# Loading each expert weight tile as two half transfers, in a two-model kernel whose experts stream from HBM

## The chip, the cores and the metric

The kernel runs on one core of one Trainium2 chip. The metric is the device time of one execution in microseconds (us), lower is better. The core has engines that run side by side: TensorE (PE in the profile; its weight loads PEld), VectorE (DVE), ScalarE (ACT), GpSimd (POOL) and SyncE (SP), which here only issues transfers; 16 DMA engines carry out what SP and POOL issue. All data are float32.

## The reference

The reference is a two-layer model followed by a second two-layer model, on 256 tokens of 1024 features. The change touches only the mixture of experts at the end of each of the second model's two layers:

```python
for g in range(N_GROUPS):            # 4 groups of 8 experts
    a = jnp.einsum('td,edf->tef', t, w_gate[sl])   # [256,1024] x [1024,512] an expert
    u = jnp.einsum('td,edf->tef', t, w_up[sl])
    act = jax.nn.silu(a) * u * combine[:, sl, None]
    out = out + jnp.einsum('tef,efd->td', act, w_down[sl])   # [512,1024] an expert
```

`combine` is nonzero for two experts of each token. Each expert has three weight matrices (gate, up, down) of 2 MB, so a layer reads 96 tiles of 2 MB, whichever tokens go where.

## The kernel before

Every engine has a program of its own, written out by hand, and waits on semaphores. A dictionary of names per semaphore (`Signal`) gives the value to wait for; `then_inc` attaches an increment to an instruction.

**Weights.** All weights go through one ring `W` of slots of 2 MB (16 KB in each of 128 partitions): six in `wring`; in the expert stage three more in `AR` (`W.widen`), nine in all. The SP program is the list of all transfers in the order of use. `fill` takes the next slot of the ring, waits until the tile that lay in it has been read (`bank`, `after`, `W.free`), and issues the transfer, which adds 16 to the slot's own semaphore (`slots`, s_w0 to s_w8). SP goes through its list strictly in order. A gate, up or down tile of an expert (`expert`) is laid out as `(p k) n -> p k n`: partition p gets k successive rows of the matrix, 16 KB that lie together in HBM and in the partition.

**Experts.** A layer takes the path `sparse` if no expert has more than 32 tokens, and it does on these inputs (the path `dense`, also edited, is not run). For each expert, in order, the PE program runs `up(ex)`: gate, then up, each 8 matmuls of 512 columns in four row groups of 32 (a float32 matmul stands twice in the trace, so 16 records a tile); `scatter(ex-1)`, which adds the result of the expert before into the output; `inner(ex)`, which folds and turns the products; every second expert `gather` for the next two; and `lower(ex)`, 8 matmuls with the down tile. The last matmul on a tile adds to `experts_read`, which is what SP waits for.

**Around it.** The first nine tiles of a layer's experts are fetched while the layer's mixers and router still run; then the ring is full and SP waits for the first gate tile to be read. After the last expert's tiles SP goes on with the next layer's matrices. Expert 31's up tile is number 94 of the 96 (counted from 0), its down tile number 95.

Of the kernel before, what the change touches and what calls it, by code (L numbers as in the profile page):

```python
# [16 lines left out]
NSLOT = 6  # L17
# [142 lines left out]
class Ring:  # L160
# [35 lines left out]
        kept = self.freed.setdefault(name, [])  # L196
        kept += [x for x in events if x not in kept]

    def ended(self, name):

        return self.freed.get(self.before.get(name), ())


def after(e, ring, name):

    for sig, key in ring.ended(name):
        e.wait_ge(sig, key)


# [84 lines left out]
def build(nc, t, out):  # L294
# [31 lines left out]
    def dma(name):  # L326
        return sig(name, 16)

    slots = [dma(f"w{i}") for i in range(NSLOT + 3)]
    W = Ring([wring[:, i * SLOT:(i + 1) * SLOT] for i in range(NSLOT)] + [AR[:, ARENA - i * SLOT:ARENA - (i - 1) * SLOT] for i in (2, 1, 3)], 3)  # L330
    PA, PB = Ring(banks[0:4]), Ring(banks[4:8])

# [49 lines left out]
    def tok(m):  # L382
        return slice(m * 128, m * 128 + 128)
# [118 lines left out]
    def blocks(place, kt, n):  # L502
        return place[:, 0:kt * n].rearrange("p (k n) -> p k n", k=kt)
# [59 lines left out]
    def sync(e):  # L563
        def fill(name, parts):
            place = bank(e, W, name)
            for dst, src in parts(place):
                e.dma_start(dst, src).then_inc(slots[W.where[name]], name)

# [2 lines left out]

        def expert(name, src, kt, n):

            fill(name, lambda place: [(blocks(place, kt, n), src.rearrange("(p k) n -> p k n", p=128))])

        def memory(layer):
            fill(("mem", layer), lambda place: [(pair(place[:, 2048:4096]), t["mem"][0].rearrange("(a p) d -> p a d", p=128))])
# [27 lines left out]
        c, c1, c2 = dma("c"), dma("c1"), dma("c2")  # L605
# [67 lines left out]
    def tensor(e):  # L673
        turned = sig("norm_mm")

        def place(name):

            e.wait_ge(slots[W.where[name]], name)
            return W[name]

        def weights(name, kt, n):
            return blocks(place(name), kt, n)

        def norm_half(tag, m):

# [774 lines left out]
        def sparse(layer):  # L1460

            done, vect, act = sig(f"moe_mm{layer}"), sig(f"moe_v{layer}"), sig(f"moe_a{layer}")
            read = sig(f"experts_read{layer}")
            PB = path_rings("sparse", layer)
            _, HG, SWT, GC, UC, AT, YS, _ = moe_rings(layer)

            def up(ex):
                p, x = ex // 2, ex % 2
                e.wait_ge(act, ("g", p))
                e.wait_ge(vect, ("g", p))  # L1470
                for name in ("gate", "eup"):
                    wx = weights((name, layer, ex), 8, 512)
                    ps = bank(e, PB, (name, ex))
                    for i in range(2):
                        for q in range(4):
                            k = 2 * q + i
                            ins = e.matmul(ps[32 * q:32 * q + 32, :], HG[p][:, k, 32 * x:32 * x + 32], wx[:, k, :], i == 0, i == 1)
                    ins.then_inc(read, (name, ex))
                    W.free((name, layer, ex), (read, (name, ex)))

            def inner(ex):

                ps = bank(e, PB, ("t", ex))
                for n, (tile, ready) in enumerate(((GC[ex], (act, ("gate", ex))), (UC[ex], (vect, ("eup", ex))))):
                    e.wait_ge(*ready)
                    for f in range(4):
                        c = 128 * n + 32 * f
                        ins = e.matmul(ps[:, c:c + 32], tile[:, f, :], C("fold", 32), True, True)
                ins.then_inc(done, ("t", ex))

            def lower(ex):
                wd = weights(("edown", layer, ex), 4, 1024)
                y = bank(e, PB, ("y", ex))
                e.wait_ge(vect, ("act", ex))
                for i in range(2):
                    for c in range(2):
                        for h in range(2):
                            r, f = 64 * c + 32 * h, 2 * h + i
                            ins = e.matmul(y[r:r + 32, :], AT[ex][:, f, :], wd[:, f, c * 512:c * 512 + 512], i == 0, i == 1)
                ins.then_inc(read, ("edown", ex))  # L1500
                W.free(("edown", layer, ex), (read, ("edown", ex)))

            def scatter(ex):
                p, x = ex // 2, ex % 2
                e.wait_ge(act, ("w", p))
                e.wait_ge(*((sig(f"join_v{layer}"), "end") if ex == 31 else (vect, ("y", ex))))
                for m in range(2):
                    for c in range(2):
                        r = slice(64 * c, 64 * c + 64)
                        ins = e.matmul(PA[("moe", layer), m, c][:, :], SWT[p][r, x, tok(m)], YS[ex][r, :], False, ex == 31)  # L1510
                if ex == 31:
                    ins.then_inc(sig(f"join_mm{layer}"), "end")
                else:
                    ins.then_inc(done, ("sc", ex))

            for ex in range(32):
                up(ex)
                if ex:
                    scatter(ex - 1)
                inner(ex)  # L1520
                if ex % 2 and ex < 31:
                    gather(layer, ex // 2 + 1)
                lower(ex)
            scatter(31)

        def dense(layer):

            done, vect, act = sig(f"dense_mm{layer}"), sig(f"dense_v{layer}"), sig(f"dense_a{layer}")
            read = sig(f"experts_read{layer}")
            PB = path_rings("dense", layer)  # L1530
            GAS, CR = dense_rings(layer)
            e.wait_ge(sig(f"moe_v{layer}"), ("g", 0))
            e.wait_ge(sig(f"moe_a{layer}"), ("w", 0))
            for m in range(2):
                for c in range(2):

                    e.matmul(PA[("moe", layer), m, c][:, 0:128], bc(C("strip", 1), 128), IDENT, False, True)
                    ps = bank(e, PB, ("ht", m, c))
                    for j in range(4):
                        k = 4 * c + j  # L1540
                        ins = e.transpose(ps[:, j * 128:j * 128 + 128], XN[:, m, k * 128:k * 128 + 128], IDENT)
                    ins.then_inc(done, ("ht", m, c))
            e.wait_ge(act, ("ht", 1, 1))
            for ex in range(32):
                ps = bank(e, PB, ("cr", ex))
                for m in range(2):
                    ins = e.matmul(ps[:, tok(m)], bc(CB[:, m, ex:ex + 1], 128), IDENT, True, True)
                ins.then_inc(done, ("cr", ex))
                wg, wu = (weights((name, layer, ex), 8, 512) for name in ("gate", "eup"))
                for f in range(4):  # L1550
                    ps = bank(e, PB, ("up", ex, f))
                    for j, wt in enumerate((wg, wu)):
                        for k in range(8):
                            ins = e.matmul(ps[:, j * 256:j * 256 + 256], wt[:, k, f:512:4], HT[:, k, :], k == 0, k == 7)
                        if f == 3:
                            ins.then_inc(read, (("gate", "eup")[j], ex))
                    if f < 3:
                        ins.then_inc(done, ("up", ex, f))
                wd = weights(("edown", layer, ex), 4, 1024)
                e.wait_ge(vect, ex)  # L1560
                for f in range(4):
                    for m in range(2):
                        for c in range(2):
                            ins = e.matmul(PA[("moe", layer), m, c][:, :], GAS[ex][:, f, tok(m)], wd[:, f, c * 512:c * 512 + 512],
                                           ex == 0 and f == 0, ex == 31 and f == 3)
                ins.then_inc(read, ("edown", ex))
            for c in range(2):
                ps = bank(e, PB, ("gate", c))
                e.matmul(ps[:, :], bc(IDENT[:, 64 * c:64 * c + 1], 128), experts_gate(layer), True, True).then_inc(done, ("gate", c))
            for m in range(2):  # L1570
                for c in range(2):
                    cs = slice(c * 512, c * 512 + 512)
                    e.wait_ge(sig(f"join_v{layer}"), "end")
                    e.matmul(PA[("moe", layer), m, c][:, :], IDENT, XN[:, m, cs], True, False)
                    ins = e.matmul(PA[("moe", layer), m, c][:, :], IDENT, X[:, m, cs], False, True)
            ins.then_inc(sig(f"join_mm{layer}"), "end")
# [1634 lines left out]
```

## Time and profile before

| | |
|---|---|
| device time, median of 3 runs | 2466.88 us (2464.61 to 2468.08) |
| the profiled execution | 2466.74 us, of which the span of the trace is 2464.9 us |
| PE busy / DVE / ACT | 2225.2 / 1084.9 / 588.8 us |
| granted TensorE clock, mean | 0.965 of full speed |
| DMA | 651.32 MB, 264 GB/s over the span |
| expert stages | about 1303 to 1745 us (layer 0) and 2009 to 2453 us (layer 1) |

Busy shares of TensorE come from modelled ends of pipelined matmuls and say little alone. What is to be read is what each engine waits for and, in the expert stages, what the DMA engines do. A packet is one contiguous piece moved by one DMA engine; the packets of a few bytes are the semaphore increments at the end of a transfer (16 of them for each transfer).

### The profile page before, as it was taken

To read this page: it belongs to the slowest core of one execution; us is meant where nothing else is said; L and a number is where in the kernel's file an instruction comes from. 1 tells how busy PE (TensorE), PEld (TensorE's weight loads), DVE (VectorE), ACT (ScalarE), POOL (GpSimd) and SP (SyncE) were. 2 spreads that over 40 slices of the span, in tenths; PEclk is the share of its full clock that TensorE was granted. 3 is DMA by queue.
4 is the path that set the end of the run, shared out by engine and by line. 5 is a ranking of instruction groups with operands and counts; after the bars stand their busy time and mean duration, and the time that the engine had idled before them with its cause. 6 is when DMAs were issued, how large, how long until landed. Compare 5 with 4: busy or idle time off the path is not lost.

```text
span 2464.9 us, 31938 instructions
## 1 busy us (share of the span) xinstructions
PE 2225.2 (90%) x12996; PEld 1453.2 (59%) x12996; DVE 1084.9 (44%) x2397; ACT 588.8 (24%) x1304; POOL 58.5 (2%) x88
## 2 busy tenths in 40 slices
PE   8999999999999999999998977878799989878776
PEld 7888869846865897468764433333568744333332
DVE  4764458883464688443443222222334342222222
ACT  4331423001243320032622111111314421111111
POOL 0010000001000000002000000000002000000000
PEclk9999999999999999999999999998899989999998
DMA  8221244496923646844258999999743559999996
GB/s 313 103 78 69 86 163 164 179 370 195 321 103 140 219 154 226 307 158 139 103 238 345 427 428 427 427 428 427 292 159 115 204 213 427 428 427 427 428 427 285
DMA packets 140910, 651.32 MB, mean 264 GB/s; under 512 B 6970, under 2 KB 13418, under 8 KB 116048
## 3 DMA queue, kind: packets, MB, share of 16 engines
q1 hardware_dynamic: 138336, 642.13, 66.0%
q0 software_dynamic: 2416, 7.02, 1.2%
q8 instruction: 107, 1.75, 0.3%
q14 instruction: 51, 0.42, 0.0%
HBM read 647.81 MB, written 1.31 MB: 263 GB/s over the span
## 4 chain that ended last, share of the span: by engine, by line
PE 61%; DMA 24%; DVE 10%; ACT 3%; issue 1%; DVEq 0%; ACTq 0%
PE ps L106 59%; DMA wring<-in_w_up 24%; DVE wring L129 2%; PE ps L109 2%; DVE AR L125 2%; DVE AR L129 1%; ACT AR L115 1%; ACT L115 1%; DVE wring L125 1%; DVE AR L120 1%; DVE AR L133 0%; ACT HT L115 0%; ACT wring L115 0%; DVE XN L121 0%; ACT MN L115 0%
## 5 line engine op out<-in xcount | busy, mean ns | idle before, releaser
L106 PE MATMUL ps<-HT,wring 128*128 128x256 f32 (+1 forms) x2848 | 532.0, 345 | 5.0 <-DVE wring L125 4.0
L106 PEld LDWEIGHTS ps<-HT,wring 128*128 128x128 f32 x2848 | 466.4, 193 | 62.7 <-issue 6.6
L106 PE MATMUL ps<-wring,AR 128*32 128x512 f32 (+3 forms) x1376 | 346.7, 614 | 18.4 <-DVE AR L125 17.2
L106 PE MATMUL ps<-wring,MN 128*32 128x512 f32 (+1 forms) x1504 | 241.3, 659 | 91.5 <-DMA wring<-in_w_up 79.8
L115 ACT ACTIVATE AR<-ps 128x128 f32<-128x128 f32 (+6 forms) x234 | 94.6, 404 | 721.2 <-PE ps L106 663.8
L106 PEld LDWEIGHTS ps<-wring,AR 128*32 128x32 f32 (+1 forms) x1376 | 134.8, 150 | 177.9 <-issue 176.0
L125 DVE TENSOR_TENSOR AR<-ps,AR 128x512 f32<-128x512 f32 (+4 forms) x200 | 100.5, 503 | 264.5 <-ACT AR L115 165.8
L106 PEld LDWEIGHTS ps<-wring,MN 128*32 128x32 f32 (+1 forms) x1504 | 68.1, 122 | 246.8 <-DMA wring<-in_w_up 120.7
L106 PE MATMUL ps<-AR 128*128 128x128 f32 (+5 forms) x1400 | 195.2, 393 | 13.5 <-DVE AR L125 10.8
L141 DVE COPY HT<-ps 128x512 f32<-128x512 f32 x64 | 44.3, 691 | 317.4 <-PE ps L106 317.4
L106 PEld LDWEIGHTS ps<-AR 128*128 128x128 f32 (+4 forms) x1400 | 137.5, 173 | 50.1 <-issue 36.5
L106 PEld LDWEIGHTS ps<-CS,HT 128*128 128x128 f32 x1024 | 119.1, 191 | 48.8 <-issue 48.8
L115 ACT ACTIVATE HT<-ps 128x512 f32<-128x512 f32 x112 | 66.9, 597 | 298.5 <-PE ps L106 297.0
L106 PE MATMUL ps<-XN,wring 128*128 128x128 f32 x1056 | 130.1, 275 | 3.0 <-DVE wring L125 2.0
L129 DVE SCALAR_TENSOR_TENSOR wring<-wring,CC 128x512 f32<-128x512 f32 x168 | 126.3, 752 | 6.0
L106 PE MATMUL ps<-CS,HT 128*128 128x32 f32 x1024 | 126.2, 277 | 0.0
L106 PEld LDWEIGHTS ps<-XN,wring 128*128 128x128 f32 x1056 | 123.7, 192 | 3.7 <-DVE wring L125 2.4
L106 PE MATMUL ps<-XN,AR 128*128 128x128 f32 (+1 forms) x656 | 114.4, 415 | 0.8 <-DVE AR L125 0.8
L106 PE MATMUL ps<-AR,MN 128*32 128x512 f32 (+1 forms) x704 | 86.5, 592 | 13.6 <-DMA AR<-in_w_gate 13.6
L125 DVE TENSOR_TENSOR MN<-ps,AR 128x512 f32<-128x512 f32 x64 | 44.3, 691 | 117.3 <-PE ps L106 117.3
L115 ACT ACT_TABLE_LOAD x66 | 84.7, 1283 | 13.4 <-DVE MN L125 8.5
L115 ACT ACTIVATE AR<-AR,PV 128x256 f32<-128x256 f32 x104 | 52.9, 508 | 131.7 <-DVE AR L125 77.0
(172 smaller groups left out, 2103.5 us busy)
## 6 DMA issues: line engine op xcount, KB each, us to landing
wring<-in_w_up SPq DMA_DIRECT2D x64, 2048.0 KB, 41.3
AR<-in_w_gate SPq DMA_DIRECT2D x42, 2048.0 KB, 39.1
wring<-in_w_down SPq DMA_DIRECT2D x42, 2048.0 KB, 36.7
wring<-in_w_ada SPq DMA_DIRECT2D x24, 2048.0 KB, 11.5
wring<-in_w_gate SPq DMA_DIRECT2D x22, 2048.0 KB, 39.4
AR<-in_w_down SPq DMA_DIRECT2D x22, 2048.0 KB, 35.9
wring<-in_ffn_w_up SPq DMA_DIRECT2D x20, 2048.0 KB, 8.0
wring<-in_w_in SPq DMA_DIRECT2D x18, 2048.0 KB, 9.7
```

Source lines behind the costliest of these rows:

```text
L106: return Ins(self.eng and self.eng.matmul(out, lhs, rhs, start=start, stop=stop), None)
L109: return Ins(self.eng and self.eng.transpose(out, in_, ident), None)
L115: return Ins(self.eng and self.eng.activation(out, in_, func, **kw), self)
L120: return Ins(self.eng and self.eng.tensor_scalar(out, in_, s1, None, op0), self)
L125: return Ins(self.eng and self.eng.tensor_tensor(out, in0, in1, op), self)
L129: return Ins(self.eng and self.eng.scalar_tensor_tensor(out, in0, s, in1, op0, op1), self)
L141: return Ins(self.eng and self.eng.tensor_copy(out, in_), self)
```

## The change

`expert` issues two transfers of 1 MB in place of one of 2 MB: the first carries the first half of each partition's rows (8 KB in each partition), the second the other half. The first half adds to the slot's semaphore as before, the second to one of nine new ones (`seconds`, s_v0 to s_v8). PE waits for the first half, does the four matmuls that read it, waits for the second, and does the other four. After its first four matmuls it releases the first half of the slot, and SP may refill it alone (`after_half`). Which rows a matmul takes changes with it: k = 4i + q in place of 2q + i, so that the first four matmuls read rows 0 to 3.

```diff
-    def ended(self, name):
-
-        return self.freed.get(self.before.get(name), ())
+    def ended(self, name, half=None):
+
+        before = self.before.get(name)
+        return self.freed.get((before, half), self.freed.get(before, ()))
...
+def after_half(e, ring, name, half):
+
+    for sig, key in ring.ended(name, half):
+        e.wait_ge(sig, key)
...
+    seconds = [dma(f"v{i}") for i in range(NSLOT + 3)]
...
-            fill(name, lambda place: [(blocks(place, kt, n), src.rearrange("(p k) n -> p k n", p=128))])
+            wt, rows = blocks(W.take(name), kt, n), src.rearrange("(p k) n -> p k n", p=128)
+            for half, landed in enumerate((slots, seconds)):
+                ks = slice(kt // 2 * half, kt // 2 * half + kt // 2)
+                after_half(e, W, name, half)
+                e.dma_start(wt[:, ks, :], rows[:, ks, :]).then_inc(landed[W.where[name]], name)
...
+        def second_rows(name, kt, n):
+            e.wait_ge(seconds[W.where[name]], name)
+            return blocks(W[name], kt, n)
...
-                    for i in range(2):
+                    for i, rows in enumerate((first_rows, second_rows)):
+                        wx = rows(tile, 8, 512)
                         for q in range(4):
-                            k = 2 * q + i
+                            k = 4 * i + q
                             ins = e.matmul(ps[32 * q:32 * q + 32, :], HG[p][:, k, 32 * x:32 * x + 32], wx[:, k, :], i == 0, i == 1)
-                    ins.then_inc(read, (name, ex))
-                    W.free((name, layer, ex), (read, (name, ex)))
+                        ins.then_inc(read, (name, ex) if i else (name, ex, 0))
+                    W.free((tile, 0), (read, (name, ex, 0)))
+                    W.free(tile, (read, (name, ex)))
...
-                            r, f = 64 * c + 32 * h, 2 * h + i
+                            r, f = 64 * c + 32 * h, 2 * i + h
```

`lower` is edited in the same way, and `dense` waits for both halves and releases the first.

SP's list at the tenth tile of layer 0 on, the first tiles for which SP waits on the experts' own reads (128x4096 is 128 partitions of 4096 numbers, 16 KB); before:

```order
L101 DMA wring<-in_w_down 128x4096
L101 DMA wring<-in_w_gate 128x4096 [waits s_experts_read0]
L101 DMA wring<-in_w_up 128x4096 [waits s_experts_read0]
L101 DMA AR<-in_w_down 128x4096 [waits s_experts_read0]
L101 DMA AR<-in_w_gate 128x4096 [waits s_experts_read0]
L101 DMA wring<-in_w_up 128x4096 [waits s_experts_read0]
```

and after:

```order
L101 DMA wring<-in_w_down 128x2048 x2
L101 DMA wring<-in_w_gate 128x2048 [waits s_experts_read0] x2
L101 DMA wring<-in_w_up 128x2048 [waits s_experts_read0] x2
L101 DMA AR<-in_w_down 128x2048 [waits s_experts_read0] x2
L101 DMA AR<-in_w_gate 128x2048 [waits s_experts_read0] x2
L101 DMA wring<-in_w_up 128x2048 [waits s_experts_read0] x2
```

The tiles stand in the same order and slots; each is two transfers of 8 KB in a partition, with a wait each.

PE's program at the first expert of layer 0, where `up(0)` reads the gate tile (s_w3) and the up tile (s_w4), and `inner(0)` follows:

```order
-L106 MATMUL ps<-wring,MN 32x512 x7
+L106 MATMUL ps<-wring,MN 32x512 x3
+L106 MATMUL ps<-wring,MN 32x512 [waits s_v3]
+L106 MATMUL ps<-wring,MN 32x512 x3
 L106 MATMUL ps<-wring,MN 32x512 [waits s_w4]
-L106 MATMUL ps<-wring,MN 32x512 x7
+L106 MATMUL ps<-wring,MN 32x512 x3
+L106 MATMUL ps<-wring,MN 32x512 [waits s_v4]
+L106 MATMUL ps<-wring,MN 32x512 x3
 L106 MATMUL ps<-CS,HT 128x32 [waits s_moe_a0]
```

No matmul is added or moved; the fifth of each eight now carries a wait of its own.

## Rows read from the trace of the kernel before

**Rows 1.** The page's head and its 40 slices of the span.
```profile
span 2464.9 us, 31938 instructions
...
PEclk9999999999999999999999999998899989999998
DMA  8221244496923646844258999999743559999996
GB/s 313 103 78 69 86 163 164 179 370 195 321 103 140 219 154 226 307 158 139 103 238 345 427 428 427 427 428 427 292 159 115 204 213 427 428 427 427 428 427 285
```

**Rows 2.** The chain of work, 1395 to 1520 us: start us, us, what.
```profile
1403.27 5.57 PE ps L106 x48
...
1408.85 42.02 DMA wring<-in_w_up
...
1450.92 1.97 PE ps L106 x16
...
1452.90 42.97 DMA wring<-in_w_up
```

**Rows 3.** PE's waits, 1310 to 1404 us: who waited for whom, us, times, longest.
```profile
PE ps L106 <- DVE AR L125: 3.1, 4, 0.8
PE ps L109 <- ACT HT L115: 2.8, 4, 0.7
```

**Rows 4.** All waits, 1404 to 1745 us, those of PE for tiles.
```profile
PE ps L106 <- DMA wring<-in_w_up: 40.3, 17, 3.9
...
PE ps L106 <- DMA AR<-in_w_gate: 8.2, 6, 1.5
...
PE ps L106 <- DMA wring<-in_w_gate: 3.6, 2, 2.3
```

**Rows 5.** DMA traffic, 1320 to 1700 us: packets by size, queues (q8: instruction fetches).
```profile
DMA packets 11151, 162.35 MB, mean 427 GB/s; under 512 B 1239, under 2 KB 1239, under 8 KB 1239
...
q1 hardware_dynamic: 11128, 162.03, 100.3%
q8 instruction: 17, 0.28, 0.3%
```

**Rows 6.** Timeline, 1282 to 1318 us: first gate and up tile read, first refills.
```profile
1302.69 3.64 PE L106 MATMUL ps<-wring,MN 128*32 128x512 f32 x32 [1.19 <-ACT MN L115]
...
1304.66 0.33 SPq L101 DMA_DIRECT2D wring<-in_w_gate  x1
...
1306.38 0.33 SPq L101 DMA_DIRECT2D wring<-in_w_up  x1
```

**Rows 7.** Timeline, 1988 to 2025 us: the same place in layer 1.
```profile
2008.82 6.06 PE L106 MATMUL ps<-wring,MN 128*32 128x512 f32 x32 [0.77 <-ACT MN L115]
...
2012.51 0.33 SPq L101 DMA_DIRECT2D wring<-in_w_gate  x1
```

**Rows 8.** Timeline, 1716 to 1757 us: the last expert of layer 0.
```profile
1732.55 2.41 PE L106 MATMUL ps<-wring,MN 128*32 128x512 f32 x16 [2.97 <-DMA wring<-in_w_up]
...
1734.89 3.15 PE L106 MATMUL ps<-MN 64*128 64x512 f32 x8
...
1740.72 3.57 PE L106 MATMUL ps<-wring,AR 128*32 128x512 f32 x16 [0.78 <-DVE AR L125]
```

**Rows 9.** Timeline, 2398 to 2466 us: the last expert of layer 1.
```profile
2425.56 1.92 PE L106 MATMUL ps<-wring,MN 128*32 128x512 f32 x16 [1.73 <-DMA wring<-in_w_up]
...
2440.24 3.54 PE L106 MATMUL ps<-wring,MN 128*32 128x512 f32 x16 [2.97 <-DMA wring<-in_w_up]
...
2443.72 2.02 PE L106 MATMUL ps<-MN 64*128 64x512 f32 x8
...
2448.42 1.92 PE L106 MATMUL ps<-wring,AR 128*32 128x512 f32 x16 [0.79 <-DVE AR L125]
```

**Rows 10.** DMA traffic, 533 to 538 us: full queue of tiles in 4 KB packets.
```profile
DMA packets 515, 2.04 MB, mean 409 GB/s; under 512 B 16, under 2 KB 16, under 8 KB 515
```

**Rows 11.** DMA traffic, 543 to 553 us: full queue of tiles in 2 KB packets.
```profile
DMA packets 1911, 3.86 MB, mean 386 GB/s; under 512 B 32, under 2 KB 32, under 8 KB 1910
```

**Rows 12.** SP's issues, 1302 to 1700 us: duration ns min/median/max; issue to landing.
```profile
L101 SPq DMA_DIRECT2D wring<-in_w_up x29: 327/328/328, 1306.4 to 1691.1; - x29
...
DMA to landing us min/median/max: 7.8/39.7/43.0
```

More of the change, by code:

```diff
@@ L682, in weights, with first_rows @@
             return blocks(place(name), kt, n)
+        def first_rows(name, kt, n):
+            return weights(name, kt, n)
+        def second_rows(name, kt, n):
+            e.wait_ge(seconds[W.where[name]], name)
+            return blocks(W[name], kt, n)
         def norm_half(tag, m):
@@ L1471, in up @@
                 for name in ("gate", "eup"):
-                    wx = weights((name, layer, ex), 8, 512)
+                    tile = name, layer, ex
                     ps = bank(e, PB, (name, ex))
-                    for i in range(2):
+                    for i, rows in enumerate((first_rows, second_rows)):
+                        wx = rows(tile, 8, 512)
                         for q in range(4):
-                            k = 2 * q + i
+                            k = 4 * i + q
                             ins = e.matmul(ps[32 * q:32 * q + 32, :], HG[p][:, k, 32 * x:32 * x + 32], wx[:, k, :], i == 0, i == 1)
-                    ins.then_inc(read, (name, ex))
-                    W.free((name, layer, ex), (read, (name, ex)))
+                        ins.then_inc(read, (name, ex) if i else (name, ex, 0))
+                    W.free((tile, 0), (read, (name, ex, 0)))
+                    W.free(tile, (read, (name, ex)))
             def inner(ex):
@@ L1491, in lower @@
             def lower(ex):
-                wd = weights(("edown", layer, ex), 4, 1024)
+                tile = "edown", layer, ex
                 y = bank(e, PB, ("y", ex))
                 e.wait_ge(vect, ("act", ex))
-                for i in range(2):
+                for i, rows in enumerate((first_rows, second_rows)):
+                    wd = rows(tile, 4, 1024)
                     for c in range(2):
                         for h in range(2):
-                            r, f = 64 * c + 32 * h, 2 * h + i
+                            r, f = 64 * c + 32 * h, 2 * i + h
                             ins = e.matmul(y[r:r + 32, :], AT[ex][:, f, :], wd[:, f, c * 512:c * 512 + 512], i == 0, i == 1)
-                ins.then_inc(read, ("edown", ex))
-                W.free(("edown", layer, ex), (read, ("edown", ex)))
+                    ins.then_inc(read, ("edown", ex) if i else ("edown", ex, 0))
+                W.free((tile, 0), (read, ("edown", ex, 0)))
+                W.free(tile, (read, ("edown", ex)))
             def scatter(ex):
@@ L1548, in dense @@
                 ins.then_inc(done, ("cr", ex))
-                wg, wu = (weights((name, layer, ex), 8, 512) for name in ("gate", "eup"))
+                for name in ("gate", "eup"):
+                    first_rows((name, layer, ex), 8, 512)
+                wg, wu = (second_rows((name, layer, ex), 8, 512) for name in ("gate", "eup"))
                 for f in range(4):
@@ L1554, in dense @@
                             ins = e.matmul(ps[:, j * 256:j * 256 + 256], wt[:, k, f:512:4], HT[:, k, :], k == 0, k == 7)
+                            if f == 3 and k == 3:
+                                ins.then_inc(read, (("gate", "eup")[j], ex, 0))
                         if f == 3:
@@ L1558, in dense @@
                         ins.then_inc(done, ("up", ex, f))
-                wd = weights(("edown", layer, ex), 4, 1024)
+                first_rows(("edown", layer, ex), 4, 1024)
+                wd = second_rows(("edown", layer, ex), 4, 1024)
                 e.wait_ge(vect, ex)
@@ L1565, in dense @@
                                            ex == 0 and f == 0, ex == 31 and f == 3)
+                    if f == 1:
+                        ins.then_inc(read, ("edown", ex, 0))
                 ins.then_inc(read, ("edown", ex))
```

## The prediction

> **What bounds the kernel now.** I read the page's slices first. In slices 23 to 28 and 34 to 39 of 40 the DMA row stands at 9 and the rate at 427 to 428 GB/s, the highest of the span; elsewhere it is mostly half or less [rows 1]. These are the two expert stages. Then the chain of work: before 1408.85 us it runs through PE, and from there on it is a DMA of 42 us, 1.97 us of PE, a DMA of 43 us, and so on [rows 2]: a slot is refilled, lands, is read, and is refilled. Nine slots in (42.02 + 1.97) us is 4.89 us for 2 MB. The waits agree: from 1310 to 1404 us PE waits for no tile [rows 3], and from 1404 to 1745 us it waits 40.3 + 8.2 + 3.6 = 52.1 us for tiles [rows 4].
>
> Next, is it the latency of one transfer or the rate of the 16 DMA engines that sets those 4.89 us? The rate: the load queue alone is busy for 100.3% of 16 engines' time and moves 427 GB/s, which is 2.097 MB in 4.91 us [rows 5]. From issue to landing it takes 39.7 us in the median, eight tiles' worth of queue, against 7.8 us at the least [rows 12]. The queue is thus about eight tiles deep and never dry. PE is no bound here: it has caught up by 1404 us and idles.
>
> So an expert stage is a stream with three parts. It starts when the first gate tile has been read and SP refills its slot (1304.66 us in layer 0 [rows 6], 2012.51 us in layer 1 [rows 7]); nine tiles are there by then and no transfer is queued. It runs without a gap through tiles 9 to 94, 86 tiles. It ends with what PE does after expert 31's up tile has landed (1732.55 us [rows 8], 2440.24 us [rows 9]). Check: 1732.55 − 1304.66 = 427.9 us and 2440.24 − 2012.51 = 427.7 us; 86 × 4.91 = 422.3 us, and the rest is the first transfer's latency and small stalls. Whatever changes the stream's start, the time of a tile in it, or the tail changes the end one for one; PE's early lead, SP's waits and DVE's and ACT's work do not.
>
> **The start of the stream: a gain.** The first gate tile's 16 records take from 1302.69 us to the refill at 1304.66 us, 1.97 us [rows 6]; in layer 1 from 2008.82 to 2012.51 us, 3.69 us, at the lower clock [rows 7]. Now the first half is released after 8 records, so its refill goes out 1.0 us and 1.8 us earlier. The second half's goes out when the whole tile's did, at most 1.8 us later, while a half keeps the DMA engines busy for 2.46 us, so no gap opens. The refill of up follows 1.72 us behind [rows 6], also in time. Gain: **2.8 us** in both layers.
>
> **The tail: a gain.** Expert 31's second half lands when the whole tile would have. By then PE has done the first four matmuls: it idles 2.97 us before this tile in both layers [rows 8, 9], and the first half lands 2.46 us earlier. 8 records are left of 16. At full clock 16 take 1.92 us, 8 take 0.96 us [rows 9]. Layer 0 spent 1734.89 − 1732.55 = 2.34 us, layer 1 2443.72 − 2440.24 = 3.48 us, since the lower level of the clock fell on them. If the low stretch stays where it is, half is saved, 1.2 and 1.7 us; if the last 8 run at full clock, 1.4 and 2.5 us; if both layers are at full clock before and after, 1.0 each. I take 1.2 and 1.7, **2.9 us**, with 1.9 to 3.9 as bounds. The down tile does not take over: it lands one tile, about 5 us, behind up, and is first read 8.17 us behind it in both layers [rows 8, 9], 5.5 us at the least with these savings.
>
> **The wait in the middle: nothing.** The other 31 experts also start on half a tile, but PE only idles in other places; the slots it frees early lengthen a queue that is already eight tiles deep. Queued behind the new waits on PE are scatter and inner, which DVE and ACT wait for; none is late, since the same last row lands. If the cover (the full queue) were gone, each tile's refill would come up to 1 us sooner; that is not the case.
>
> **SP: nothing.** It issues 96 more transfers a layer at 0.33 us [rows 12], 0.66 us a tile against 4.91 us. Its only neighbour in the queue is itself; POOL issues nothing there. The new waits sit on matmuls that stood there before, and the added DMA instructions must be fetched: 17 fetches went by in 380 us [rows 5]. One or two more a layer, each at most about a packet of the same size on one of 16 engines (0.6 us), give 0 to 2 us in all. I take 0.
>
> **The packets: a loss.** In the stage 11151 − 1239 = 9912 packets move 162.35 MB, 16.4 KB each: one partition's row of a tile is one packet [rows 5]. The change cuts it into two of 8 KB. This trace has no tile in 8 KB packets, so I bound their price by full queues at other sizes. The time of a packet on one of the 16 engines is 16 × size / rate: 16 × 16384 / 427 = 613.9 ns [rows 5]; 16 × 4096 / 409 = 160.2 ns [rows 10]; 16 × 2048 / 386 = 84.9 ns [rows 11]. For the same 16 KB these are 613.9, 4 × 160.2 = 641, and 8 × 84.9 = 679 ns. Three packets more cost 27 ns, 9.0 each; four more cost 38 ns, 9.6 each. Two intervals that far apart give the same price, so a packet costs about 9.3 ns whatever its size, and 8 KB lies between measured points. A tile has 8 rows an engine, so it gets 8 packets more, 74 ns; the second semaphore increment is one small packet more an engine, 0 to 9 ns (I take 5). 79 ns × 86 tiles × 2 layers = **13.6 us**. The lower bound is 0, if the price vanished above 4 KB (9.0 against 9.6 leaves room for a small fall, not for that); the upper, 9.6 × 9 × 172 = 14.9 us.
>
> The Trainium skill has a figure for this, "DMA: Bandwidth & Descriptors", section "Why small descriptors are slow": a fixed overhead of about 3 cycles a packet inside a DMA engine, at an 850 MHz fabric, which it calls worth removing only up to 256 B. An estimate from that page: 3.5 ns × 8 × 172 = 4.9 us in place of 13.6, and the total would be about 0.8 us faster than before. The rows speak against it as the whole cost: they show 9.0 to 9.6 ns.
>
> **Sum.** −2.8 − 2.9 + 13.6 = +7.9 us. The profiled execution took 2466.74 us, its span and 1.8 us around it, and lies 0.14 us below the median of the runs; on the median I get 2466.9 + 7.9 = **2474.8 us**, 0.32% slower. The halves would pay off below 5.7 / 172 = 33 ns a tile, 4 ns a packet.
>
> **The rivals.**
> - **Packets nearly free (same).** A DMA engine loses a few cycles at each packet and the rest of the 9.3 ns goes with the size: the rate stays at about 424 GB/s. At half the price of the rows 6.8 − 5.7 = +1 us, at a quarter 3.4 − 5.7 = −2 us: 2465 to 2468 us. For it: nothing between 4 and 16 KB was measured. Against it: the equal slopes. Chance 0.23. The Trainium skill's page named above would put it here, at its estimate of −0.8 us.
> - **No price at all (faster).** The other side: two 8 KB packets take as long as one of 16 KB, the stream keeps 427 GB/s, and start and tail remain: −5.7 us, 2461.2 us. It decides from 4 ns a packet down; it needs under 0.5 ns to pass the bound of 0.2% (4.9 us, about what a measurement of this kernel can tell), or a tail that recovers its clock. Chance 0.09.
> - **Half rows read badly (much slower).** Each half now reads 8 KB at a stride of 16 KB. If that cost as much as cutting to 4 KB does, a tile would take 2.097 MB / 409 GB/s = 5.13 us, 0.22 us more: 37 us less 5.7, 2498 us. For it: only that no such pattern was timed; 2 KB pieces of wider rows reach the rate of the line above. Chance 0.06.
> - **The forecast.** +4.9 to +13 us. Chance 0.62.
>
> **How the numbers follow.** The likeliest case's own range is 2470 (a third of the packet price off) to 2481 us (14.9 + 2 − 4.7 = +12.2 us, and two more for runs). For 8 in 10 it must reach into the first rival, down to 2465 us, and leave out the second and the third: 2465 to 2481 us. Faster 0.09; within 0.2% 0.25, the first rival and the forecast's lower edge; slower 0.66.
>
> **What the profile after would show.** Right: in 1320 to 1700 us twice the packets for the same bytes and 420 to 422 GB/s; the first refill about 1 us (layer 0) and 1.8 us (layer 1) sooner after the first matmul; from first refill to expert 31's up about 434 us a layer; 8 records behind the last landing. Wrong: 425 GB/s or more, or a DMA share below 99% there, which would mean that the queue ran dry. My forecast falls if the price of a packet is not constant between 4 and 16 KB, or if the clock at the start and the tails moves by more than the 1 to 2 us that I gave it.

## The result, and the profile after

The change makes the kernel slower: 2473.41 us in the median of 11 runs (2469.14 to 2479.24), against 2466.79 us (2462.67 to 2469.24) for the kernel before in the same rounds. The ratio is 1.0033, 95% interval 1.0022 to 1.0043, which is 8.1 us (5.4 to 10.6). The profiled execution took 2478.84 us, at the slow end of the runs, so its tails are not typical (below).

The page's head and slices of the changed kernel, against [rows 1]:

```profile
span 2477.0 us, 32130 instructions
...
DMA  8221244596924546834259999999752569999996
GB/s 312 102 77 69 86 166 168 180 369 189 312 102 153 204 154 250 305 135 137 102 237 382 420 421 421 421 421 421 278 170 103 204 262 421 421 420 422 420 421 259
```

The expert stages are as full as before, but at 420 to 421 GB/s in place of 427 to 428. The DMA traffic from 1320 to 1700 us, against [rows 5]:

```profile
DMA packets 21943, 159.94 MB, mean 421 GB/s; under 512 B 2437, under 2 KB 2437, under 8 KB 2437
...
q1 hardware_dynamic: 21920, 159.61, 101.0%
q8 instruction: 17, 0.28, 0.3%
```

21943 − 2437 = 19506 packets for 159.94 MB are 8.2 KB each, at a share of 101.0%: the engines are not short of work, each 16 KB takes longer. Instruction fetches are 17 as before. The start of the stream in both layers (timeline), against [rows 6, 7]:

```profile
1303.60 3.64 PE L106 MATMUL ps<-wring,MN 128*32 128x512 f32 x32 [1.19 <-ACT MN L115]
...
1304.71 1.31 SPq L101 DMA_DIRECT2D wring<-in_w_gate  x2
...
2013.58 3.64 PE L106 MATMUL ps<-wring,MN 128*32 128x512 f32 x32 [1.19 <-ACT MN L115]
...
2014.69 1.19 SPq L101 DMA_DIRECT2D wring<-in_w_gate  x2
```

The first refill leaves 1.11 us after the first matmul in both layers, where it took 1.97 and 3.69 us. The last expert's up tile, against [rows 8, 9]:

```profile
1736.60 1.07 PE L106 MATMUL ps<-wring,MN 128*32 128x512 f32 x8 [1.42 <-DMA wring<-in_w_up]
...
1739.09 1.94 PE L106 MATMUL ps<-wring,MN 128*32 128x512 f32 x8 [1.43 <-DMA wring<-in_w_up]
...
2446.89 1.06 PE L106 MATMUL ps<-wring,MN 128*32 128x512 f32 x8 [1.90 <-DMA wring<-in_w_up]
...
2449.39 1.93 PE L106 MATMUL ps<-wring,MN 128*32 128x512 f32 x8 [1.43 <-DMA wring<-in_w_up]
```

PE reads half a tile, waits 1.4 us, and has 8 records left when the rest lands. From first refill to this landing it is 1739.09 − 1304.71 = 434.4 us and 2449.39 − 2014.69 = 434.7 us, against 427.9 and 427.7 us before: 6.5 and 7.0 us longer, for 86 tiles 75 and 81 ns a tile.

### The profile page after: what moved, and what is told of

It reads as the page before. It is cut to its first block, busy times and chain, and to the rows that moved or that the text cites. A ratio compares the mean times of both kernels' runs of the same rounds, so it can differ in the third digit from the quotient of the medians.

```text
span 2477.0 us, 32130 instructions
## 1 busy us (share of the span) xinstructions
PE 2242.3 (91%) x12996; PEld 1446.0 (58%) x12996; DVE 1085.4 (44%) x2397; ACT 589.0 (24%) x1304; POOL 58.5 (2%) x88
## 4 chain that ended last, share of the span: by engine, by line
PE 59%; DMA 26%; DVE 10%; ACT 3%; issue 1%; SPq 1%; DVEq 0%; ACTq 0%
PE ps L106 57%; DMA wring<-in_w_up 26%; DVE wring L129 2%; PE ps L109 2%; DVE AR L125 2%; ACT AR L115 1%; DVE AR L129 1%; SPq L101 1%; ACT L115 1%; DVE wring L125 1%; DVE AR L120 1%; DVE AR L133 0%; ACT HT L115 0%; ACT wring L115 0%; DVE XN L121 0%
## 5 line engine op out<-in xcount | busy, mean ns | idle before, releaser
L106 PEld LDWEIGHTS ps<-wring,MN 128*32 128x32 f32 (+1 forms) x1504 | 61.0, 119 | 256.9 <-DMA wring<-in_w_up 159.2
L106 PE MATMUL ps<-AR 128*128 128x128 f32 (+5 forms) x1400 | 199.4, 406 | 11.1 <-DVE AR L125 8.3
L106 PE MATMUL ps<-AR,MN 128*32 128x512 f32 (+1 forms) x704 | 90.6, 606 | 11.3 <-DMA AR<-in_w_gate 11.1
```

What stands on the lines that cost most here:

```text
L106: return Ins(self.eng and self.eng.matmul(out, lhs, rhs, start=start, stop=stop), None)
```

## The experiments

Names below are those of the runs without their number. "Stretch" is the time from the stage's first refill to the read of the last up tile.

**1. split_only.** The transfers are cut, TensorE waits for both halves before it reads, and both wait for the whole tile before them:

```diff
-                after_half(e, W, name, half)
+                after(e, W, name)
...
         def first_rows(name, kt, n):
+            e.wait_ge(seconds[W.where[name]], name)
             return weights(name, kt, n)
```

> Two transfers of 8 KB rows for each expert tile, but TensorE waits for both before it reads, and both wait for the whole tile before them to be read: the change without its early read and early release. Theory A (a fixed price of about 9.3 ns for each packet): 13.6 us slower than before, about 2480 us, 421 GB/s in the stream, and some 6 us slower than the full change, whose start and tail gain that. Theory B (the loss of the full change came from its extra waits and from refilling singly, and packets are nearly free): within 2 us of before, 425 GB/s or more.

Measured: 2478.52 us, ratio 1.0045 (1.0028 to 1.0061), and the DMA traffic of the changed kernel (1320 to 1700 us):

```profile
DMA packets 21943, 159.94 MB, mean 421 GB/s; under 512 B 2437, under 2 KB 2437, under 8 KB 2437
```

Theory A holds, theory B falls: the loss is there without any early read or release. It is 11.1 us (6.9 to 15.1) where 13.6 were expected. By the ratios this is 3 us slower than the full change where 6 were expected; the two intervals overlap.

**2. partition_halves.** The halves are partitions 0 to 63 and 64 to 127, so rows stay whole:

```diff
-                ks = slice(kt // 2 * half, kt // 2 * half + kt // 2)
-                e.dma_start(wt[:, ks, :], rows[:, ks, :]).then_inc(landed[W.where[name]], name)
+                ps = slice(64 * half, 64 * half + 64)
+                e.dma_start(wt[ps, :, :], rows[ps, :, :]).then_inc(landed[W.where[name]], name)
```

> Also two transfers of 1 MB and two semaphores for each tile, both waited for together, but one carries partitions 0 to 63 and the other 64 to 127, so each row stays one packet of 16 KB. Theory A (price per packet): within 2 us of before, 426 to 427 GB/s; only the second semaphore packet is left, at most 1.5 us. Theory C (the price is per transfer, not per packet): as slow as with 8 KB rows, about 13 us slower than before, 421 GB/s.

Measured: 3280.95 us, ratio 1.3297, outside every theory. Traffic from 1320 to 1700 us:

```profile
DMA packets 6275, 82.25 MB, mean 216 GB/s; under 512 B 1253, under 2 KB 1253, under 8 KB 1253
```

Packets of 16 KB as before, at half the rate. This tells nothing between A and C, so run 8 was made.

**3. quarters.** Four transfers of 512 KB, rows of 4 KB, all waited for together:

```diff
+            for part, landed in enumerate((slots, slots, seconds, seconds)):
+                ks = slice(kt // 4 * part, kt // 4 * part + kt // 4)
```

> Four transfers of 512 KB for each tile, each with a quarter of every partition's rows (4 KB packets), all waited for together. Theory A (9.3 ns for each packet, 24 more on each engine for a tile): 24 x 9.3 ns = 223 ns for a tile plus three more semaphore packets at 5 ns, 238 ns x 172 = 41 us slower than before, about 2508 us, 408 GB/s. Theory D (the price grows faster than the number of packets): over 50 us slower.

Measured: 2501.56 us, ratio 1.0139 (1.0120 to 1.0158), 34 us slower. Traffic from 1320 to 1700 us, then the timeline at the first refill and at the last up tile of layer 0:

```profile
DMA packets 42608, 155.40 MB, mean 409 GB/s; under 512 B 4730, under 2 KB 4730, under 8 KB 42584
```
```profile
1306.57 1.75 SPq L101 DMA_DIRECT2D wring<-in_w_gate  x4
...
1753.61 2.67 PE L106 MATMUL ps<-wring,MN 128*32 128x512 f32 x16 [3.20 <-DMA wring<-in_w_up]
```

409 GB/s is the rate of whole 2 MB transfers in 4 KB packets [rows 10]. The stretch is 447.0 us, 19.1 more than before: 222 ns a tile for 24 packets more, 9.3 ns each, beside 238 ns expected. The price is the same for 8 more and for 24 more, so theory D falls. The device time grew by 34 us (30 to 39), which fits twice 19.1 us; 41 were expected.

**4. order_only.** The kernel before, with `k = 4 * i + q` and `f = 2 * i + h`.

> The kernel before with one edit: the matmuls read rows 0 to 3 first (k = 4i + q, f = 2i + h); transfers and waits as before. All theories: no difference, within 1 us. A difference would mean that the order in which the rows are read costs something by itself.

Measured: 2465.73 us, ratio 0.9994 (0.9977 to 1.0011), 427 GB/s. The stretches are 428.8 and 427.9 us, as before. No cost of the order is seen, though the interval of the whole time reaches from 5.7 us faster to 2.7 us slower.

**5. read_early.** split_only's transfers (`after` for both), with the early read of the full change.

> Two transfers of 8 KB rows; TensorE reads the first half as soon as it has landed, but both halves of a slot are refilled only when the whole tile has been read. Theory A (stream price about 13 us, start gain 2 to 3 us from the early release, tail gain 2 to 3 us from the early read): the stream of split_only and the tail gain alone, 2 to 3 us faster than split_only, about 10 us slower than before. Theory B (early read costs, through more waits and more idle of TensorE): as slow as split_only or slower.

Measured: 2472.45 us, ratio 1.0028 (1.0018 to 1.0039), 6.9 us (4.4 to 9.6) slower than before, where about 10 were expected; by the ratios 4 us faster than split_only, which ran in other rounds. Theory B falls by the next run, release_early, which reads no tile early and took 5.4 us more in the same rounds. Both differences are larger than the computed 2 to 3 us. The last up tile of layer 0:

```profile
1737.83 1.07 PE L106 MATMUL ps<-wring,MN 128*32 128x512 f32 x8 [1.43 <-DMA wring<-in_w_up]
...
1740.32 1.07 PE L106 MATMUL ps<-wring,MN 128*32 128x512 f32 x8 [1.42 <-DMA wring<-in_w_up]
```

**6. release_early.** The full change with split_only's `first_rows`: both halves are waited for before the read.

> Two transfers of 8 KB rows; the first half of a slot is released and refilled after the first four matmuls, but TensorE starts on a tile only when both halves are there. Theory A: the stream begins 1 us sooner in each layer (1.8 us where the low clock falls on it), so 2 to 3 us faster than split_only, about 10 us slower than before. Theory B (refilling singly costs through SP's queue): as slow as split_only or slower.

Measured: 2479.05 us, ratio 1.0050 (1.0037 to 1.0063), no faster than split_only. Its first refill did leave 1.12 us after the first matmul (1309.08 to 1310.20 us), 0.85 us sooner than before. From the first gate matmul to the read of the last up tile, layer 0 took 435.3 us against 436.4 in split_only. So the trace has the gain at the start, about 1 us; the whole time, with intervals of 3 us and more to either side, can't show it, and a gain of 2 to 3 us is not seen.

**7. two_tiles.** A test on the name decides which tiles are cut:

```diff
+    def cut(name):
+        tile, layer, ex = name
+        return (tile, ex) in (("gate", 3), ("eup", 31))
...
+            if not cut(name):
+                after(e, W, name)
+                e.dma_start(wt, rows).then_inc(slots[W.where[name]], name)
+                return
```

> Only two tiles of each layer are loaded in halves: expert 3's gate tile, the first refill of the stage, and expert 31's up tile, the last that TensorE waits for. All others are whole transfers with 16 KB rows. Theory A: the price of the packets falls away (4 tiles x 79 ns = 0.3 us), start and tail keep their gain: 4 to 5 us faster than before, about 2462 us, at 427 GB/s. Theory B (the gains were never there; the full change was only less slow than computed): within 1 us of before.

Measured: 2460.18 us, ratio 0.9985 (0.9974 to 0.9996), 3.7 us (1.0 to 6.4) faster than before, where 4 to 5 were expected; 427 GB/s. Start and last up tile of layer 0:

```profile
1303.93 3.64 PE L106 MATMUL ps<-wring,MN 128*32 128x512 f32 x32 [1.19 <-ACT MN L115]
...
1305.05 1.19 SPq L101 DMA_DIRECT2D wring<-in_w_gate  x2
...
1733.28 1.06 PE L106 MATMUL ps<-wring,MN 128*32 128x512 f32 x8 [1.43 <-DMA wring<-in_w_up]
```

The stretch is 428.2 us, as before. The gains exist, and without the packets' price they show as a faster kernel: theory B falls here.

**8. one_transfer.** One transfer a tile, with each partition's 16 KB from two places of the matrix. The partitions hold the weight rows in another order, so the products are not the reference's; the amount of work is the same.

```diff
-[(blocks(place, kt, n), src.rearrange("(p k) n -> p k n", p=128))]
+[(blocks(place, kt, n).rearrange("p (h k) n -> p h k n", h=2),
+  src.rearrange("(h p k) n -> p h k n", h=2, p=128))]
```

> One transfer and one semaphore for each expert tile as before, but each partition's 16 KB come from two places of the matrix, 8 KB each, so every row is two packets of 8 KB. The partitions hold the weight rows in another order, so the products are not the reference's; the work is the same. Theory A (price per packet): 421 to 422 GB/s and 12 to 13 us slower than before, like split_only. Theory C (price per transfer): 427 GB/s, no slower than before.

Measured: 2480.27 us, ratio 1.0054 (1.0041 to 1.0067), 13.3 us slower. Traffic from 1320 to 1700 us:

```profile
DMA packets 20731, 159.97 MB, mean 421 GB/s; under 512 B 1221, under 2 KB 1221, under 8 KB 1221
```

Half the semaphore packets of the changed kernel (1221 for 2437), the same rate. The price is the packets', not the transfers'. Theory C falls.

**9 to 12.** The changed kernel again, and three choices of tiles to cut: only expert 31's up tile; only expert 3's gate tile; both of these and all of experts 30 and 31.

> The changed kernel as it is, on the same chip and in the same rounds as the three below, with a second profile of it. In its first profile both tails ran largely at the lower clock and took 25.5 and 27.6 us, against 21.9 and 22.1 us in the profile of read_early, whose tails hold the same instructions. Theory A (the early release gains about 1 us a layer, and the spread of 10 us between runs is the clock in the tails): a tail without low stretches takes about 22 us, and the stretch from the first gate matmul to the last up half stays at 435 to 436 us a layer. Theory E (the full change makes the tails slow by itself): they are at 25 us or more again.

> Only expert 31's up tile is loaded and read in halves, in each layer; everything else as before. Theory A: the eight matmul records left behind the landing save 1 us a layer at the full clock, up to 1.7 us at the low one, 2 to 3 us together, against 4 to 6 us for the two tiles of two_tiles. Theory F (the tail's gain is mostly the clock: a TensorE that works in the last wait keeps its clock for the rest of the tail): nearly all of two_tiles' gain, 4 to 5 us, with tails of 22 us in the profile.

> Only expert 3's gate tile, the first refill of the stage, is loaded in halves and its first half refilled early. Theory A: the stream starts 0.9 us sooner in a layer at full clock, 1.8 us at the low one: 2 to 3 us faster than before. Theory F: less than 2 us, and the rest of two_tiles' gain stands with the tail tile.

> The tiles of two_tiles and all tiles of experts 30 and 31 in halves, 7 of 96 in a layer. The packet price is 14 x 0.08 = 1.1 us. Theory A: 4 us faster than before, 1 us less than two_tiles. Theory F: the clock is kept up in more of the runs, so as fast as two_tiles or 1 to 2 us faster.

| run | median us | ratio, 95% interval |
|---|---|---|
| full_again | 2474.81 | 1.0039 (1.0026 to 1.0052) |
| tail_tile | 2462.28 | 0.9991 (0.9980 to 1.0001) |
| start_tile | 2460.79 | 0.9981 (0.9972 to 0.9990) |
| last_experts | 2458.99 | 0.9983 (0.9970 to 0.9995) |

The tails, from the read of the last up tile (or its second half) to the next layer's first projection, and in layer 1 to the end of the span. Each row: stretch, its length us, busy time and count of PE, PEld, DVE, ACT, POOL, then the granted clock, DMA share and GB/s. Before, changed kernel, full_again, read_early and split_only, in this order:

```profile
1732.55:1758.65 26.10, 16.64 (x80) 8.04 (x81) 8.60 (x23) 7.68 (x17) 0.00 (x0) 0.72 1.04 382
2440.24:2464.90 24.66, 11.30 (x64) 4.35 (x64) 9.17 (x23) 4.99 (x11) 0.00 (x0) 0.78 0.19 78
```
```profile
1739.09:1764.63 25.54, 17.95 (x72) 8.22 (x73) 8.61 (x23) 7.68 (x17) 0.00 (x0) 0.63 1.05 384
2449.39:2477.00 27.61, 14.34 (x56) 4.93 (x56) 9.17 (x23) 4.99 (x11) 0.00 (x0) 0.62 0.16 65
```
```profile
1740.73:1764.41 23.68, 14.30 (x73) 7.46 (x73) 8.61 (x23) 7.69 (x17) 0.00 (x0) 0.79 1.04 383
2448.97:2472.70 23.73, 10.43 (x56) 3.98 (x56) 9.17 (x23) 4.99 (x11) 0.00 (x0) 0.76 0.19 77
```
```profile
1740.32:1762.22 21.90, 12.49 (x72) 7.03 (x73) 8.60 (x23) 7.70 (x17) 0.00 (x0) 0.85 1.04 387
2447.32:2469.40 22.08, 8.80 (x56) 3.81 (x56) 9.18 (x23) 4.99 (x11) 0.00 (x0) 0.84 0.21 83
```
```profile
1740.86:1763.65 22.79, 13.36 (x81) 7.29 (x81) 8.61 (x23) 7.70 (x17) 0.00 (x0) 0.83 1.05 385
2451.89:2476.70 24.81, 11.30 (x64) 4.36 (x64) 9.18 (x23) 4.99 (x11) 0.00 (x0) 0.79 0.19 77
```

The same instructions take 21.90 us where the mean granted clock is 0.85 and 25.54 us where it is 0.63. In the profiles of runs 9 to 12 layer 0's tail took 23.7, 23.5, 22.7 and 24.9 us. Theory E falls: the changed kernel's tails are not slow by themselves (its second profile has 23.7 us twice). Theory A's 435 to 436 us from the first gate matmul to the last up half came in layer 1 of that profile (435.8 us) and not in layer 0 (437.8 us), whose start lay at the low clock. Theory A's share of the tail is 22.79 − 21.90 = 0.9 us, read off two layer 0 tails whose clock was high. Theory F is neither shown nor excluded for the tail: tail_tile alone gained 2.2 us, with an interval from 0.2 us slower to 4.9 us faster that holds both theories, and last_experts and two_tiles can't be told apart. Its other half falls: start_tile should have gained less than 2 us and gained 4.7 us (2.5 to 6.9), where theory A computed 2 to 3. The four choices, 0.9981 to 0.9991, can't be told apart by their intervals; three of the four exclude "no gain", and tail_tile does not.

## Why the prediction was right

The forecast was 2474.8 us, 7.9 us slower; measured were 2473.4 us and a ratio worth 8.1 us, and 9.6 us the second time. The mechanism was the one forecast, and the terms came out as follows.

- **The stream sets the time.** Right. Cut transfers without any gain gave 421 GB/s and cost 11 to 13 us (split_only, one_transfer); their stretches grew by 6.5 and 6.5 us, and 6.8 and 6.8 us, 13.0 to 13.6 us for the two layers.
- **The packets, +13.6 us.** Right in kind and nearly in size: 434.4 − 427.9 and 434.7 − 427.7 make 13.5 us with the full change, and 9.3 ns a packet holds at 4 KB too. The 5 ns for the second increment are not seen: one_transfer has none and grew no less than split_only. The equal slopes between 2, 4 and 16 KB in the trace before carried this term; the experiments filled in the 8 KB between. The rival "packets nearly free", and with it the figure of the Trainium skill ("DMA: Bandwidth & Descriptors", "Why small descriptors are slow"), falls: as the whole cost, an estimate of 3.5 ns a packet from its 3 cycles, it would have been 4.9 us, and the runs show 2.7 times that. So do "no price at all" and "half rows read badly" (421 GB/s, no slower with a stride of 16 KB than with the two places of one_transfer).
- **The start, −2.8 us.** The place was right, and at each level of the clock the size nearly: 0.86 us at the full clock (1.97 to 1.11 us), where 1.0 was forecast, and 1.7 us at the lower one (3.69 to 1.98 us), where it was 1.8. That second figure is from layer 0 of full_again:

```profile
1302.90 5.95 PE L106 MATMUL ps<-wring,MN 128*32 128x512 f32 x32 [0.77 <-ACT MN L115]
...
1304.88 2.03 SPq L101 DMA_DIRECT2D wring<-in_w_gate  x2
```

What the prediction could not know from one profile is where the low clock lies. It took it to stay on layer 1's start. In other profiles it lay on layer 0's start (full_again, quarters), on both (last_experts), or on neither (the changed kernel's first, order_only, read_early).
- **The tail, −2.9 us.** The same: the 8 records are 0.9 us a layer at full clock, and the rest was the clock of that one profile. Start and tail by their instructions at full clock are 1.7 + 1.8 = 3.5 us, not 5.7. two_tiles gained 3.7 us net, in line with this; start_tile's 4.7 us for the start alone is not, and why is open.
- **The sum.** With these terms it is 13.5 − 3.5 = +10.0 us. That lies in both intervals of the changed kernel (5.4 to 10.6 and 6.4 to 12.8 us), but it is not the forecast 7.9: that the forecast came within 0.2 us of the first measured 8.1 is in part luck. The early release is also not seen in the whole times: the changed kernel, 8.1 and 9.6 us slower, is no faster than read_early, 6.9 us slower, which goes without it. The traces alone show its gain (435.5 and 435.8 us from the first gate matmul to the last up half, 436.3 and 436.5 us in read_early).
- **The clock.** Given 1 to 2 us in the prediction, it moved the two tails of single executions by up to 5.5 us (27.61 against 22.08 us). It is the likeliest source of the spread of 10 us between the changed kernel's runs. The mean clock granted in each of the 11 runs agrees: 0.957 to 0.959 in the four slowest (2477.9 us and more), 0.961 to 0.964 in the four fastest. Where in the run the clock was low is known for the profiled runs only.
- **SP: nothing.** The outcome was right, the working wrong. The prediction had each issue at 0.33 us. SP's issues in the changed kernel, 1302 to 1700 us, duration ns min/median/max, and issue to landing, against [rows 12]:

```profile
L101 SPq DMA_DIRECT2D wring<-in_w_up x56: 327/2132/6427, 1306.4 to 1695.6; - x56
...
DMA to landing us min/median/max: 5.1/27.0/30.9
```

SP is held 2.1 us at each issue, and a half waits 27 us for its landing, 11 halves at 2.5 us: the queue takes no more than about 11 of them, where before eight whole tiles stood in it. From about 1372 us on SP's issues follow one another without a pause, so SP is late with its list, but 27 us of queue are still ahead of the DMA engines (share 101%), so nothing waits for it. It also means that a slot that is released early in mid-stage is not refilled early; the early release can only matter at the first refill, when the queue is empty.

## What to carry to other kernels

Where a queue of transfers is never dry, count its packets: here each packet more cost 9 to 10 ns on its engine at every size between 2 and 16 KB, and a finer hand-over that halves contiguous rows pays that for every tile. Cut only the transfers that something waits for: the first refill of a stage, which goes out to an empty queue, and the last tile that the stage waits for. Here that gave 2 to 5 us of 2466. And before a term is read off one profile, see whether the low clock lay on it.

## What the runs showed that was not expected

- Transfers of 64 partitions in place of 128, one behind the other on one queue, ran at 216 GB/s against 427, with the same 16 KB packets and a share of the DMA engines near 100%: 16 × 16384 / 216 = 1214 ns a packet in place of 614. What limits them was not tried; two such transfers do not run as one.
- SP is held once about 11 transfers of 1 MB are queued. With quarters of 512 KB it is held 1.08 us an issue in the median and the landing comes after 15.1 us, 12 transfers. Both have 9 packets an engine for each transfer, with the increment's. That the limit goes by packets and not by transfers is seen in one_transfer, whose whole 2 MB transfers have 17 packets an engine (SP's issues, 1302 to 1700 us):

```profile
L101 SPq DMA_DIRECT2D wring<-in_w_up x28: 367/4617/10912, 1307.0 to 1691.9; - x28
...
DMA to landing us min/median/max: 7.7/32.9/39.5
```

SP is held 4.6 us an issue with only 32.9 / 4.98 = 6.6 transfers queued, while the kernel before had 8 whole transfers of 9 packets queued and SP was not held (0.33 us). In packets on each engine the three held cases are 98, 106 and 112, the one not held 73: an estimate from these rows is a queue of about 100 to 110 packets an engine.
